# The second MLP's alternating loop with the down product ahead of the up product in each pair

## The reference, cut to what matters

```python
h2 = rmsnorm(x, mlp_norm_g[l])
x = x + jnp.square(jax.nn.relu(h2 @ w_ff1[l])) @ w_ff2[l]
```

## Time and profile before

| | us |
|---|---|
| Median of 3 runs | 2825.39 |
| Lowest, highest | 2823.96, 2837.76 |
| The profiled execution | 2830.28 |
| Its span | 2828.5 |
| TensorE busy in the span | 2736.8 (97%) |
| VectorE, GpSimd, ScalarE busy | 1656.2, 1177.0, 935.8 |
| The alternating loop, from the first unit to the last | 2242.1 to 2743.0 |

### The profile page before, as it was taken

The page is one execution under the profiler, slowest core; times in us unless marked ns, Lnnn a source line. Parts: engine busy times, 40 slices in busy tenths (PEclk is TensorE's granted clock), DMA queues, the critical chain, the costliest instruction groups (busy, mean ns, idle before and its releaser), DMA issues.

```text
span 2828.5 us, 36638 instructions
## 1 busy us (share of the span) xinstructions
PE 2736.8 (97%) x14424; PEld 2186.8 (77%) x14424; DVE 1656.2 (59%) x2218; ACT 935.8 (33%) x1490; POOL 1177.0 (42%) x665
## 2 busy tenths in 40 slices
PE   7999999999999999999999999999999999999998
PEld 4888887788888888776788656666887788888876
DVE  4843234653333233564899933699457577777763
ACT  5001124432110003355222166665114344444443
POOL 1443333454444444443122213010334777777862
PEclk9999999999999999999999999999999999999999
DMA  8531114233111113335133200000431122221122
GB/s 316 174 124 45 38 38 134 87 93 91 52 51 45 52 46 97 88 111 146 30 86 99 68 13 2 2 2 2 164 112 45 45 68 61 67 68 56 56 71 97
DMA packets 252055, 215.07 MB, mean 76 GB/s; under 512 B 23915, under 2 KB 228218, under 8 KB 251514
## 3 DMA queue, kind: packets, MB, share of 16 engines
q1 hardware_dynamic: 248874, 204.53, 23.5%
q10 hardware_dynamic: 3024, 8.39, 0.8%
HBM read 190.87 MB, written 20.97 MB: 75 GB/s over the span
## 4 chain that ended last, share of the span: by engine, by line
PE 76%; DVE 16%; ACT 3%; issue 3%; POOL 1%; DMA 0%; SPq 0%; ACTq 0%; DVEq 0%; POOLq 0%
PE PS L1223 14%; PE PS L1453 10%; PE PS L1798 9%; PE PS L1832 8%; DVE MB L3093 6%; PE PS L1510 6%; PE PS L1500 6%; PE PS L1469 5%; PE PS L1739 3%; PE PS L1207 3%; PE PS L1646 2%; PE PS L1704 2%; PE PS L1872 1%; DVE STEP L3195 1%; PE PS L1677 1%
## 5 line engine op out<-in xcount | busy, mean ns | idle before, releaser
L967 POOL TENSOR_TENSOR WLO<-RAW,WHI 128x1024 fp32r<-128x1024 f32 x112 | 269.8, 2410 | 475.2 <-ACT WHI L1982 475.2
L954 POOL TENSOR_TENSOR WHI<-RAW,ZERO 128x1024 fp32r<-128x1024 f32 x80 | 154.9, 1936 | 690.5 <-PE PS L1223 237.8
L1982 ACT ACTIVATE WHI<-RAW 128x1024 fp32r<-128x1024 f32 x112 | 118.7, 1060 | 468.7 <-PE PS L1453 196.0
L1223 PE MATMUL PS<-H,WHI 128*128 128x512 f32 x864 | 271.1, 395 | 2.5 <-DVE L L3242 0.9
L1223 PE MATMUL PS<-L,WHI 128*128 128x512 f32 x864 | 267.4, 391 | 0.0
L1223 PE MATMUL PS<-H,WLO 128*128 128x512 f32 x864 | 267.1, 390 | 0.0
L3406 DVE TENSOR_TENSOR X<-X,PS 128x1024 f32<-128x1024 f32 x182 | 214.6, 1213 | 6.4 <-PE PS L1832 4.5
L956 POOL TENSOR_TENSOR WLO<-RAW,WHI 128x1024 fp32r<-128x1024 f32 x80 | 211.7, 2647 | 6.3
L1080 POOL TENSOR_TENSOR QLO<-QRAW,QHI 128x512 fp32r<-128x512 f32 x116 | 171.0, 1474 | 79.4 <-ACT QHI L2314 79.2
L1453 PE MATMUL PS<-H,WHI 128*128 128x512 f32 x496 | 197.5, 398 | 4.9 <-POOL WLO L967 4.3
L1453 PE MATMUL PS<-L,WHI 128*128 128x512 f32 x496 | 194.6, 392 | 0.0
(11 more groups left out here) (462 smaller groups left out, 6099.9 us busy)
## 6 DMA issues: line engine op xcount, KB each, us to landing
RAW<-w_fc SPq DMA_DIRECT2D x96, 512.0 KB, 3.7
RAW<-w_in SPq DMA_DIRECT2D x62, 512.0 KB, 4.0
DOWNRAW<-w_ff SPq DMA_DIRECT2D x81, 256.0 KB, 2.6
ADA<-w_ada SPq DMA_DIRECT2D x32, 512.0 KB, 4.6
QRAW<-w_ff SPq DMA_DIRECT2D x32, 512.0 KB, 4.0
RAW<-w_out SPq DMA_DIRECT2D x24, 512.0 KB, 4.0
ADA_FIRST<-w_ada SPq DMA_DIRECT2D x16, 512.0 KB, 9.6
X<-x_scratch SPq DMA_DIRECT2D x2, 4096.0 KB, 13.1
```

Of the source, the lines that this page charges most:

```text
L954: nc.gpsimd.tensor_add(WHI[j][:, 0:n], RAW[j][:, 0:n], ZERO[:, 0:1].to_broadcast([P, n])).then_inc(s_whi, 1)
L967: nc.gpsimd.tensor_sub(WLO[w % 2][:, :], RAW[w % 2][:, :], WHI[w % 2][:, :].bitcast(F32)).then_inc(s_w, 1)
L1223: last = mm(bank(b + t), wt[:, k, :], half(a, (k + at) % KC, t), start=(k == 0 and n == 0), stop=(k == KC - 1 and n == 2))
```

## The change

In each pair of the loop the down product now stands first. TensorE's loop calls `pair_down(g, j)` before `pair_unit(g + 1, j)`; `up_unit` and `down_unit` swap even and odd places; `done` counts a down product's second half one unit earlier; GpSimd's low parts and sums, ScalarE's high parts of weights and SP's loads follow the new numbers. ScalarE's steps on hidden values keep their places among the numbers, and VectorE's program is the same. The diff, cut to its core:

```diff
@@ up_unit, down_unit, done
-                return FIRST_CYCLE + CYCLE * (g - 2) + 2 * j
+                return FIRST_CYCLE + CYCLE * (g - 2) + 2 * j + 1
...
-            return 7 + SECOND.index(("d", n)) if g == 0 else FIRST_CYCLE + CYCLE * (g - 1) + 2 * n + 1
+            return 7 + SECOND.index(("d", n)) if g == 0 else FIRST_CYCLE + CYCLE * (g - 1) + 2 * n
...
-            halves = min(max(n + 1 - FIRST_CYCLE, 0) // 2, 7 * (LAST_G - 1))
+            halves = min(max(n + 2 - FIRST_CYCLE, 0) // 2, 7 * (LAST_G - 1))
@@ SP
-                load_up(g + 2, 0)
                 if more:
                     sp.wait_ge(s_w, MLP2 + down_unit(g, 5) + 1)
                     load_down(g + 1, "22")
-                load_up(g + 2, 1)
+                load_up(g + 2, 0)
                 if more:
                     sp.wait_ge(s_w, MLP2 + down_unit(g, 6) + 1)
                     load_down(g + 1, "12")
+                load_up(g + 2, 1)
@@ GpSimd, the start of a cycle
+                down_sum(g, 0)
+                down_low(g, 0)
                 up_sum(u, 0)
                 up_low(u, 0)
-                down_sum(g, 0)
-                down_low(g, 0)
...
@@ TensorE
                 for j in range(7):
+                    pair_down(g, j)
                     pair_unit(g + 1, j)
-                    pair_down(g, j)
@@ ScalarE
                     if at % 2:
+                        up_high(g + 2, at // 2)
+                    else:
                         down_high(g + 1, at // 2)
-                    else:
-                        up_high(g + 2, at // 2)
```

More of the change, by code:

```diff
@@ L575, in build @@
         for g in range(1, LAST_G):
-            SUM_ORDER += [("u", g + 1, 0), ("d", g, 0), ("u", g + 1, 1), ("d", g, 1), ("d", g, 3), ("u", g + 1, 2),
-                          ("u", g + 1, 3), ("d", g, 2)]
+            SUM_ORDER += [("d", g, 0), ("u", g + 1, 0), ("d", g, 1), ("d", g, 3), ("u", g + 1, 1), ("u", g + 1, 2),
+                          ("d", g, 2), ("u", g + 1, 3)]
         SUM_ORDER += [("u", PAIR_GROUPS2 - 1, i) for i in range(4)]
@@ L1174, in _ @@
                 u = g + 1
+                down_sum(g, 0)
+                down_low(g, 0)
                 up_sum(u, 0)
                 up_low(u, 0)
-                down_sum(g, 0)
-                down_low(g, 0)
-                up_sum(u, 1)
-                up_low(u, 1)
                 down_sum(g, 1)
@@ L1183, in _ @@
                 down_low(g, 1)
+                up_sum(u, 1)
+                up_low(u, 1)
+                down_low(g, 2)
                 up_low(u, 2)
                 up_sum(u, 2)
-                down_low(g, 2)
+                down_low(g, 3)
+                down_sum(g, 2)
                 up_low(u, 3)
                 up_sum(u, 3)
-                down_low(g, 3)
-                down_sum(g, 2)
+                down_low(g, 4)
                 up_low(u, 4)
-                down_low(g, 4)
+                down_low(g, 5)
                 up_low(u, 5)
-                down_low(g, 5)
+                down_low(g, 6)
                 up_low(u, 6)
-                down_low(g, 6)
             up_alone(PAIR_GROUPS2 - 1)
```

## The result

| | before | after |
|---|---|---|
| Median, us | 2826.31 | 3228.52 |
| Lowest to highest | 2823.96 to 2837.76 | 3220.38 to 3232.14 |
| Span of the profiled execution | 2828.5 | 3228.7 |
| Mean granted clock of TensorE | 0.989 | 0.939 |

The changed kernel takes 1.141 times as long (95% interval 1.139 to 1.1429): 402 us more. The forecast was 3171 us, 346 us more, with a range of 3095 to 3255. The mechanism held, and its size came out 57 us too small.

What follows compares the result with a forecast made beforehand. TensorE was taken as the bound. Waits of 256 us plus 99 of slow clock less 9 made 346 us on the profiled 2830: 3176, and 3171 us for the median, 5 lower; range 3095 to 3255.

Steps and rivals of the forecast that it cites:

- The bound: In the second MLP's alternating loop TensorE has work throughout, so any time it stands is added to the end.
- The five chains: From end of up products u2-u6 to down products d3-d6, next d0: waits 3.4, 3.4, 4.75, 4.9, 3.5; 256 us.
- the last cycle as equal: The last cycle's group is read by other steps of the same kinds; its waits were taken as equal, without d0's.
- d4's low part: VectorE's step before d4, taken at 0.68 us; the other end, 1.0 us more in 13 to 39 places, 13 to 40.
- a sign against me: In the profile after, the prediction is wrong if the releaser of the waits is GpSimd's low part or a load.
- The clock: After each of 64 waits TensorE's matmuls run slowly: 1.55 us each, 99 us; ends nothing and 174 us.
- The sum of what goes: TensorE's 8.9 us of standing before the down products lie under the new waits: -9 us.
- GpSimd, SP: Up weights' second half loads one unit later, costed at nothing; if the cover were gone, 35 us.
- The entry: Where the loop is entered: between -6.4 and +6.5 us, taken as 0.
- Only the long gaps cost: Rival: the clock falls only at d5 and d6, 26 times, 40 instead of 99 us: 3112 us; chance 0.15.
- It never comes back: Rival: the clock stays low inside the cycle, 182 units at half rate, some 437 us: 3510 us; chance 0.08.
- Not slower: Rival: the waits never bind, 2811 us; would hold only if VectorE's order had been changed too; chance 0.06.

Runs made afterwards that it cites:

- The run with the low parts ahead: The changed kernel with VectorE's lo2, lo3 and lo4 moved ahead of reading u2, u3 and u4, additions left behind it: 3189.00 us.
- the filled kernel: The changed kernel with extra matmuls on TensorE before d3, d4, d5, d6 and the next d0, while it would stand: 3104.26 us.
- the same kernel shifted by 1.8 us: The kernel before with VectorE's new order, plus eight more matmuls once before d2 of group 5: 2855.33 us in one run.

## Why the prediction was right, and where its size was off

- *The bound.* TensorE was the bound, and every wait was added to the end. Right: 389 of the 402 us come back when the waits go, with VectorE's order changed.
- *The five chains.* Right in place, releaser and length: d3, d5, d6 and d0 within 0.04 us. They add up, one after another: without d3's the others stay as they are. Taking the last cycle as equal was wrong: its gaps are 3.24, 5.68, 7.04 and 4.07 us. Yet from its `twelve_begun` to group 15's it took 23.0 us more than before (58.50 against 35.50), and I had 22.65 for it. That is luck: this stretch holds one unit less in the new order, and before, some 3 us of waits stood in it (35.50 less twelve units of 2.72).
- *d4's low part.* Mis-sized. I took 0.68 us, because ScalarE's steps keep their order. VectorE's and GpSimd's timelines after, first at this place and then at d3:

```profile
2405.27 1.77 DVE L3396 TENSOR_TENSOR HL_T<-HV_T,HH_T 128x512 fp32r<-128x512 f32 x1
...
2394.76 0.68 DVE L3396 TENSOR_TENSOR HL_T<-HV_T,HH_T 128x512 fp32r<-128x512 f32 x1
```

```profile
2405.22 1.27 POOL L1080 TENSOR_TENSOR QLO<-DOWNRAW,QHI 128x512 fp32r<-128x512 f32 x1 [7.41 <-ACT QHI L2314]
...
2394.78 1.79 POOL L1080 TENSOR_TENSOR QLO<-DOWNRAW,QHI 128x512 fp32r<-128x512 f32 x1 [3.23 <-ACT QHI L2314]
```

GpSimd's subtraction began 0.05 us earlier, and the low part took 1.77 us, the other end of the price that I had written down; at d3 VectorE began 0.02 us ahead (2394.76 against 2394.78), took 0.68, and GpSimd's step took 1.79. It is so in all twelve full cycles. That is 1.09 us more in each cycle, 13 us. The Trainium skill (SBUF — State Buffer, "SBUF: two separate sides") says that the port the two share is an exclusive lock which the one that starts first holds for its whole instruction; these two pairs agree. In the cycle above the profile names GpSimd as d4's releaser, which I had called a sign against me. It does so in four of the twelve cycles; in the other eight, with the same gap, it names VectorE's addition:

```profile
2478.60 0.71 PE L1832 MATMUL PS<-HH_T,QHI 128*128 128x512 f32 x1 [4.32 <-DVE X L3406]
```

In all twelve a GpSimd step and the first half of the addition end within 0.01 us of each other (here 2408.18 and 2408.17), so the name tells nothing. By the program's order GpSimd's steps of that moment make the low parts of d5 and u5, and d4 starts 0.15 us after the half addition has ended. The run with the low parts ahead took 1.69 us out of the wait.
- *The clock.* This is the term that was off: 1.55 us for a gap from two single gaps, against 2.16 in the mean of the loop (10.81 / 5). 12 cycles with 10.81 us instead of 7.75 are 37 us more. The bounds that I wrote, 0 and 2.72, hold the mean, but not the whole spread (up to 3.0). One gap read from a trace was one sample of 1.4 to 3.0 us, and the two at hand were both low.
- *The sum of what goes.* I took off 8.9 us. The cycles before were only 0.18 us above 38.08, 2 us in all; the source view counts weight loads and matmuls that waited together (the weight loads have 6.4 of the 8.9, the matmuls 2.4), and waits outside these cycles. That is 7 us. Together 13 + 37 + 7 = 57 us, which is what was missing.
- *GpSimd, SP.* Costed at nothing, right: with the old load order nothing changes. The cover that I named, the waits themselves, was real: without them the new order of weights costs 1.13 us a cycle, some 14 us, well under the 35 that I had as its price. That it is the load, reached through u6's high part, is shown for the 0.71 us a cycle (39.39 to 38.68) that went when this part was made earlier; for the other 0.42 it stays open.
- *The entry.* Taken at 0. From group 1's `twelve_begun` to the first of the loop it is 47.62 us before and 47.65 after. But this stretch holds one unit more in the new order (d2), 2.72 us, so the entry itself gained that much: TensorE stands 1.95 us before d0 with 1.7 of clock behind it, where it stood 4.95 with 1.43. This miss and the one in the last cycle nearly cancel.
- *The rivals.* "Only the long gaps cost" fell: every gap of 3.23 and 3.37 us cost the clock, and those of 2.63 us did too. The limit that the Trainium skill sets (TensorE: Matmul & The Clock Gate, "HAM oscillation"), a gap length that must be passed before the clock falls, is not borne out here. Its picture of a loop that pays the slow clock in every round does agree, with 0.82 of granted clock. "It never comes back" fell with the granted clock, back at 1.00 within two units of each gap. "Not slower" was given the condition that VectorE's order changes too, and that was right; but the kernels so made take 2829 to 2839 us, within 0.4% of the kernel before, and not 2811.

## What to carry to other kernels

When two alternating streams swap places, count the units between a product's end and the first instruction that waits for anything queued behind its reading, on every in-order engine: the swap took that distance from two units to none, and VectorE and GpSimd with a quarter of each cycle to spare did not help. An order on one engine belongs to the order on another: either both are changed or neither. A price for the clock taken from one or two gaps is a sample; take the spread of all gaps in the trace as its bounds, and look for filling work where a wait can't go.

## What was not expected of the hardware

The clock's cost after a gap is not a function of its length. Gaps of 2.67 us cost 0.1 us in 12 of 12 cycles of one kernel and 1.73 us in one of the same kernel shifted by 1.8 us; gaps of 2.63 us cost 1.64 to 1.74 in another; one of 1.86 us, in the last cycle of the filled kernel, cost 1.70; gaps of 4.73 us cost from 1.4 to 3.0. After the shorter gaps the fall often comes only when the matmuls run again. And whether GpSimd's step started 0.05 us ahead of a 128x512 low part or 0.02 us behind it went, in all twelve cycles, with 1.77 or 0.68 us for the low part.
